# One pass over all tokens in eight time phases, with the depthwise conv on full 128x128 matmuls through DRAM

## The reference, cut to what matters

```python
u = rmsnorm(h, g_mix)                       # 2176 tokens x 1024 per core
proj = einsum('ntd,de->nte', u, w_in)       # 1024 -> 9216, nine parts of 1024
s  = a_c * a_h                              # branch A, conv over 3 tokens
ya = (a_b * dwconv3(s) * silu(a_z)) @ w_out_a
v  = b_v * sigmoid(b_g)                     # branch B, conv over 31 tokens
c  = dwconv31(v) + b_conv_b
yb = (silu(layernorm(c)) * silu(b_z)) @ w_out_b
m  = sigmoid(gate_a) * ya + sigmoid(gate_b) * yb
h  = h + m @ w_o
h  = h + sigmoid(rmsnorm(h, g_ple) @ w_pg) * (p @ w_pe)
y  = rmsnorm(h, g_final)
```

## Time and profile before

| | us |
|---|---|
| median of the runs (1200.08 to 1239.26) | 1201.93 |
| the profiled execution, its own time | 1197.04 |
| its span on the slowest core, first to last instruction | 1195.5 |
| spans of the eight cores | 1174.0 to 1195.5 |

### The profile page before, as it was taken

The page is one execution under the profiler, slowest core; times in us unless marked ns, Lnnn a source line. Parts: engine busy times, 40 slices in busy tenths (PEclk is TensorE's granted clock), DMA queues, the critical chain, the costliest instruction groups (busy, mean ns, idle before and its releaser), DMA issues.

```text
span 1195.5 us, 20798 instructions; the slowest of 8 cores (1174.0 to 1195.5 us)
## 1 busy us (share of the span) xinstructions
PE 1022.0 (85%) x6774; PEld 571.8 (48%) x6774; DVE 560.9 (47%) x927; ACT 356.6 (30%) x661; POOL 230.1 (19%) x512
## 2 busy tenths in 40 slices
PE   1599979989899876999988989988689978789984
PEld 1355555545466333555654546633355544445542
DVE  1334325666333454443665633345646466642354
ACT  3122231332211454223223221135422322331243
POOL 3111011212122122111221212112222222222010
PEclk9788878989999996999999989998799999989998
DMA  8675465536466342545554545543356455477221
GB/s 202 103 139 95 83 151 124 88 55 103 78 103 97 88 120 79 97 87 127 89 87 73 93 75 97 97 109 99 92 114 129 90 102 90 77 151 127 49 87 62
DMA packets 65307, 119.74 MB, mean 100 GB/s; under 512 B 8657, under 2 KB 23377, under 8 KB 64657
## 3 DMA queue, kind: packets, MB, share of 16 engines
q0 software_dynamic: 41184, 75.06, 39.3%
q1 hardware_dynamic: 24017, 43.36, 11.7%
HBM read 172.23 MB, written 11.14 MB: 153 GB/s over the span
## 4 chain that ended last, share of the span: by engine, by line
PE 66%; DVE 11%; issue 8%; ACT 7%; DMA 6%; SPq 0%; DVEq 0%; POOL 0%; ACTq 0%; POOLq 0%
PE ps L687 13%; PE ps L571 11%; PE ps L790 10%; PE ps L508 9%; PE ps L891 6%; PE ps L779 5%; PE ps L784 5%; PE ps L643 3%; DMA t_R<-t_vext 3%; PE ps L844 3%; DMA t_xs<-x 2%; ACT t_tmp L661 2%; DVE t_cbuf L663 2%; DVE t_tmp L653 2%; DVE t_tmp L721 1%
## 5 line engine op out<-in xcount | busy, mean ns | idle before, releaser
L687 PE MATMUL ps<-t_uT,t_ring 128*128 128x512 bf16 (+2 forms) x1536 | 259.3, 332 | 40.4 <-ACT t_tmp L661 23.2
L687 PEld LDWEIGHTS ps<-t_uT,t_ring 128*128 128x128 bf16 x1536 | 145.2, 102 | 152.9 <-issue 66.0
L288 POOL DMA_DIRECT2D t_ring<-w_in x216 | 115.7, 536 | 500.0 <-PE ps L508 228.5
L571 PE MATMUL ps<-t_R,t_Wp 128*64 128x512 bf16 (+2 forms) x1536 | 141.9, 341 | 15.8 <-DMA t_R<-t_vext 15.7
L508 PE MATMUL ps<-t_uT,t_ring 128*128 128x512 bf16 (+2 forms) x768 | 136.5, 336 | 0.3 <-DVE t_uT L426 0.3
L790 PE MATMUL ps<-t_uT,t_ring 128*128 128x512 bf16 (+2 forms) x768 | 129.5, 322 | 0.0
L571 PEld LDWEIGHTS ps<-t_R,t_Wp 128*64 128x64 bf16 x1536 | 84.2, 116 | 71.3 <-issue 34.1
L891 PE MATMUL ps<-t_wpg_t,t_u2T 128*128 128x512 bf16 x272 | 74.0, 434 | 31.5 <-DVE t_u2T L867 22.5
L508 PEld LDWEIGHTS ps<-t_uT,t_ring 128*128 128x128 bf16 x768 | 70.2, 102 | 63.2 <-issue 32.0
L790 PEld LDWEIGHTS ps<-t_uT,t_ring 128*128 128x128 bf16 x768 | 71.1, 99 | 51.0 <-issue 5.4
L801 DVE TENSOR_TENSOR t_tmp<-ps,t_tmp 128x512 f32<-128x512 f32 (+2 forms) x48 | 25.6, 534 | 123.9 <-ACT t_tmp L797 123.9
(11 more groups left out here) (119 smaller groups left out, 1125.3 us busy)
## 6 DMA issues: line engine op xcount, KB each, us to landing
t_ring<-w_in POOLq DMA_DIRECT2D x216, 256.0 KB, 5.2
t_xs<-x SPq DMA_DIRECT2D x34, 512.0 KB, 4.5
y<-t_yt SPq DMA_DIRECT2D x17, 512.0 KB, 2.7
t_R<-t_vext SPq DMA_DIRECT2D x96, 67.8 KB, 2.0
t_ring<-w_oa POOLq DMA_DIRECT2D x24, 256.0 KB, 4.0
t_ring<-w_ob POOLq DMA_DIRECT2D x24, 256.0 KB, 4.7
t_R<-t_vexts SPq DMA_DIRECT2D x32, 76.0 KB, 4.1
t_R<-t_vext SPq DMA_DIRECT2D x64, 35.8 KB, 3.8
```

The costliest lines, as they stand in the source:

```text
L288: S.add("pool", lambda e, k=k, src=src: e.dma_start(out=ring[k].rearrange("p k m -> p (k m)"), in_=src), writes=[f"ring{k}", swq()], dma=f ...
L571: S.add("pe", lambda e, bc=bc, ds=ds, i=i, g=g, rhs=rhs, n=n: e.matmul(ps[64 * g:64 * g + 64, bc, 0:n], lhsT=Wp[ds][:, 16 * g + i, :], rhs ...
L687: S.add("pe", lambda e, b=b, kw=kw, k=k, off=off, n=n: e.matmul(ps[:, b, 0:n], lhsT=ring[kw][:, k, :], rhs=uT[:, k, off:off + n], start=(k ...
```

## The change

All 2176 tokens go through each stage together, in five chunks (`CHUNKS`), so each weight tile is loaded once. The host lays the 2048 prompt tokens out in eight phases: token 8m + a stands at column 256a + m. A shift by eight tokens is then a shift by one column within a phase.

The long conv works on `v8`, whose 128 partitions are 16 channels x 8 phases. For 16 channels, one 128 x 128 matrix per lag (five lags) maps the eight phases of the input to the eight of the output; 64 such groups of channels times five lags make 320 matmuls of 336 columns (256 of the prompt, 80 of the short sequences with their histories). VectorE builds the matrices from a table `tw` and a block mask, four groups at a time (`w_build`). v is written to DRAM with channels as rows (`vd`, `vsd`), read back as 16 channels x 8 phases (`conv_load`), and the result makes the same way back (`cd`, `csd`, `conv_back`). The sums for the LayerNorm are then made from the result (`acc`), and the conv bias is added where it is used.

The tile of short sequences comes first. The first four channel groups are projected chunk by chunk while token tiles arrive; the other four alternate with halves of the conv. Branch A's short conv takes its earlier tokens from the phase before, so chunk 3 comes first in each j. b_z chunks stand behind j = 2 to 7. The last stage runs over 17 token tiles with more buffers, u2T of the next tile ahead of the products of this one. Each accumulation now waits for its own bank. p, and the histories, come transposed from the host; kept rows go out untransposed. The float32 identity, the halos and their copies are gone. SBUF is laid out by hand, with tiles of late stages over those of early ones (`alias` carries the waits).

The diff at its core:

```diff
+NPH = 8
+NBL = 256
+NQ = 8
+NLAG = 5
+NWIN = 336
+CHUNKS = [(0, 512), (512, 512), (1024, 512), (1536, 512), (2048, 128)]
...
+            add_group([wcol(5, j), wcol(4, j)])
...
+        TILES = [16] + list(range(16))
+        def s1_load(i):
+            t = TILES[i]
+            sdma(xs1[i % NXS][:], x_d[128 * t:128 * t + 128, :], [], [f"x1{i % NXS}"], f"x1{i % NXS}")
+        s1_load(0)
+        sdma(vecs[:], vecs_d, [], ["vecs"], "vecs")
+        for i in range(1, NXS):
+            s1_load(i)
+        pdma(idb[:], ident_d, [], ["idb"], "idb")
+        pump(2)
+        S.add("pool", lambda e: e.memset(mhalf[:], -0.5), writes=["mhalf"])
+        pump(6)
+        pdma(tw.rearrange("p a b -> p (a b)"), tw_d, [], ["tw"], "tw")
+        pdma(mask[:], mask_d, [], ["mask"], "mask")
+        S.add("pool", lambda e: e.memset(epsc[:], LN_EPS), writes=["epsc"])
...
+        def s2_proj(j, si):
+            off, n = CHUNKS[si]
+            if j not in s2w:
+                s2w[j] = wgroup()
+            g, (kg, kv) = s2w[j]
+            bg, bv = balloc(), balloc()
+            proj(bg, kg, si)
+            proj(bv, kv, si)
+            tg = talloc()
+            S.add("act", lambda e: e.activation(out=tmp[tg][:, 0:n], in_=ps[:, bg, 0:n], func=AF.Sigmoid),
+                  reads=[f"ps{bg}"], writes=[f"tmp{tg}"])
+            if si < 4:
+                q = vst_ctr[0] % NVST
+                vst_ctr[0] += 1
+                S.add("dve", lambda e: e.tensor_tensor(out=vst[q][:], in0=ps[:, bv, :], in1=tmp[tg][:], op=ALU.mult),
+                      reads=[f"ps{bv}", f"tmp{tg}"], writes=[f"vst{q}"])
...
+                sdma(vd[j][:, off:off + n], vst[q][:], [f"vst{q}"], [f"vd{j}_{si}"], f"vst{q}")
+            else:
+                S.add("dve", lambda e: e.tensor_tensor(out=vkeep_s[:, j, :], in0=ps[:, bv, 0:n], in1=tmp[tg][:, 0:n],
+                                                       op=ALU.mult),
+                      reads=[f"ps{bv}", f"tmp{tg}"], writes=[f"vkeep_s{j}"])
+                pdma(vsd[j], vkeep_s[:, j, :], [f"vkeep_s{j}"], [f"vsd{j}"], f"vsd{j % 4}")
+            bfree(bg, bv)
+        def conv_load(j):
+            s = j % 2
+            pdma(v8[s][:, :, 260:340], h8_d[j], [], [f"v8{s}h"], f"v8{s}h")
+            sdma(v8[s][:, :, 4:260], vd[j].rearrange("c (a m) -> (c a) m", m=NBL).rearrange("(q r) m -> r q m", r=128),
+                 [f"vd{j}_{si}" for si in range(4)], [f"v8{s}p"], f"v8{s}p")
+            sdma(vs8[s][:], vsd[j].rearrange("c (a m) -> (c a) m", m=16).rearrange("(q r) m -> r q m", r=128),
+                 [f"vsd{j}"], [f"vs8{s}"], f"vs8{s}")
+            S.add("pool", lambda e: e.tensor_copy(out=v8[s][:, :, 264:340:5], in_=vs8[s][:]),
+                  reads=[f"vs8{s}"], writes=[f"v8{s}h"])
+        def w_build(j, hh):
+            w = (2 * j + hh) % NWP
+            c0 = (j * NQ + 4 * hh) * NLAG
+            S.add("dve", lambda e: e.tensor_tensor(
+                out=Wp[w].rearrange("p a (c b) -> p a c b", b=NPH),
+                in0=mask.rearrange("p (c b) -> p c b", b=NPH).unsqueeze(1).to_broadcast([128, 4 * NLAG, 16, NPH]),
+                in1=tw[:, c0:c0 + 4 * NLAG, :].unsqueeze(2).to_broadcast([128, 4 * NLAG, 16, NPH]), op=ALU.mult),
+                reads=["tw", "mask"], writes=[f"Wp{w}"])
...
+        def conv_half(j, hh):
+            s, w = j % 2, (2 * j + hh) % NWP
+            for pr in range(2):
+                b0, b1 = balloc2()
+                for u, b in enumerate((b0, b1)):
+                    qq = 2 * pr + u
+                    q = 4 * hh + qq
+                    for d in range(NLAG):
+                        S.add("pe", lambda e, b=b, qq=qq, q=q, d=d: e.matmul(
+                            ps[:, b, 0:NWIN], lhsT=Wp[w][:, qq * NLAG + d, :], rhs=v8[s][:, q, 4 - d:4 - d + NWIN],
+                            start=(d == 0), stop=(d == NLAG - 1)),
+                            reads=[f"Wp{w}", f"v8{s}z", f"v8{s}p", f"v8{s}h"], writes=[f"ps{b}"])
+                x = c8_ctr[0] % NC8
+                c8_ctr[0] += 1
+                q0 = 4 * hh + 2 * pr
+                S.add("act", lambda e, b0=b0, b1=b1, x=x: e.activation(out=c8[x][:], in_=two(b0, b1, 0, NBL),
+                                                                       func=AF.Copy),
+                      reads=[f"ps{b0}", f"ps{b1}"], writes=[f"c8{x}"])
+                S.add("act", lambda e, b0=b0, b1=b1, q0=q0: e.activation(out=c8s[s][:, q0:q0 + 2, :],
+                                                                         in_=two(b0, b1, 260, NWIN, 5), func=AF.Copy),
+                      reads=[f"ps{b0}", f"ps{b1}"], writes=[f"c8s{s}"])
+                bfree(b0, b1)
+                rows = cd[j].rearrange("c (b m) -> (c b) m", m=NBL).rearrange("(q r) m -> r q m", r=128)
+                sdma(rows[:, q0:q0 + 2, :], c8[x][:], [f"c8{x}"], [f"cd{j}_{q0}"], f"c8{x}")
+            if hh == 1:
+                sdma(csd[j].rearrange("c (b m) -> (c b) m", m=16).rearrange("(q r) m -> r q m", r=128), c8s[s][:],
+                     [f"c8s{s}"], [f"csd{j}"], f"c8s{s}")
+            k = 2 * j + hh + NWP
+            if k < 2 * NCH:
+                w_build(k // 2, k % 2)
+        def conv_back(j):
+            if j == 4:
+                S.alias([f"c{q}_{si}" for q in range(4, 8) for si in range(5)], X1_RES)
+            sdma(cb[:, j, 0:2048], cd[j], [f"cd{j}_{q}" for q in (0, 2, 4, 6)], [f"c{j}_{si}" for si in range(4)],
+                 f"cb{j % 2}")
+            sdma(cb[:, j, 2048:NTOK], csd[j], [f"csd{j}"], [f"c{j}_4"], f"cbs{j % 2}")
...
+        def s6_Cpe(t):
+            x = t % 2
+            g0, g1 = balloc2()
+            e0, e1 = balloc2()
...
+            rs_ap, rs_res = s6[t]
+            S.add("act", lambda e: e.activation(out=B[x].rearrange("p (h d) -> p h d", h=2), in_=two(g0, g1, 0, 512),
+                                                func=AF.Sigmoid, scale=rs_ap),
+                  reads=[f"ps{g0}", f"ps{g1}", rs_res], writes=[f"B{x}"])
+            bfree(g0, g1)
+            return e0, e1
+        def s6_Cend(t, eb):
+            e0, e1 = eb
+            x, q = t % 2, t % 3
+            bv = B[x].rearrange("p (h d) -> p h d", h=2)
+            S.add("dve", lambda e: e.tensor_tensor(out=bv, in0=two(e0, e1, 0, 512), in1=bv, op=ALU.mult),
+                  reads=[f"ps{e0}", f"ps{e1}", f"B{x}"], writes=[f"B{x}"])
+            bfree(e0, e1)
+            S.add("dve", lambda e: e.tensor_tensor(out=B[x][:], in0=B[x][:], in1=A[q][:], op=ALU.add),
+                  reads=[f"B{x}", f"A{q}"], writes=[f"B{x}"])
...
+        s1_stats(0)
+        s1_stats(1)
+        s1_rest(0)
+        w_build(0, 0)
+        nxt = [1]
+        def s1_next():
+            i = nxt[0]
+            if i >= len(TILES):
+                return
+            nxt[0] += 1
+            if i + 1 < len(TILES):
+                s1_stats(i + 1)
+            s1_rest(i)
+        for j in range(4):
+            s2_proj(j, 4)
+            s1_next()
+        for si in range(4):
+            for j in range(4):
+                s2_proj(j, si)
+                if si == 3:
+                    wdone(s2w[j][0])
+                s1_next()
+                if si == 0 and j < NWP - 1:
+                    w_build((j + 1) // 2, (j + 1) % 2)
+                if si == 3 and 1 <= j < 3:
+                    conv_load(j - 1)
+        jobs = [(j, si) for j in range(4, 8) for si in range(5)]
+        halves = [(j, h) for j in range(NCH) for h in range(2)]
+        hk = [0]
+        accd = [0]
+        def half():
+            j, h = halves[hk[0]]
+            hk[0] += 1
+            conv_half(j, h)
+            if h == 0 and j >= 1:
+                conv_back(j - 1)
+            if h == 1:
+                if j + 2 < NCH:
+                    pend.append(j + 2)
+                if j >= 2:
+                    acc(j - 2)
+        pend = []
+        for i, (j, si) in enumerate(jobs):
+            s2_proj(j, si)
+            if si == 4:
+                wdone(s2w[j][0])
+            while pend and (pend[0] < 4 or pend[0] < j or (pend[0] == j and si == 4)):
+                conv_load(pend.pop(0))
+            while hk[0] < 14 and 1.25 * hk[0] + 1 <= i:
+                half()
+        while hk[0] < 14:
+            half()
+        while pend:
+            conv_load(pend.pop(0))
...
+        NT = NTOK // 128
+        for t in range(NT):
+            eb = s6_Cpe(t)
+            if t + 2 < NT:
+                s6_p(t + 2)
+            if t + 1 < NT:
+                s6_B(t + 1)
+            s6_Cend(t, eb)
+            if t + 2 < NT:
+                s6_A(t + 2)
+            if t + 3 < NT:
+                s6_x(t + 3)
+            s6_out(t)
```

1234 lines of the change are left out of this document (517 added, 717 removed).

## The result

The changed kernel takes 1025.26 us (median of four runs: 1016.22, which is the profiled one, 1018.01, 1032.51 and 1038.43). Without the executions that a low clock on part of the cores made longer, the ratio to the kernel before is 0.8537, with a 95% interval of 0.8267 to 0.8807. The interval is wide because the kernel before ran only four times beside it, with 1182.69 as the lowest; beside the later experiments it took 1183.06 to 1188.58 us in 21 of 22 runs, so the change is worth about 168 us. The direction was right and the time lies in the range, which is 170 us wide, but 972 was too low: the profiled span is 1014.7 us where the sum said 968.

A forecast was written before the change was run, and what follows sets the result against it. TensorE, busy 85% of the span, was taken as the bound. Work 855 + start 42 + conv path 16 + statistics 5 + z chain 10 + last stage and tail 15 + clock 25 = 968 us span, forecast 972, range 905 to 1075.

The forecast's parts named there:

- the sum of columns: TensorE work of the whole kernel, added up from matmul rates: 855 us in the new kernel, 949 in the old.
- The build's price: One Wp build of 2560 elements on VectorE: 2.9 us, or 1.5 if 16-bit inputs double the rate.
- the entry: Entry into the last stage: a loss of 5 us, beside 10 for the tail.
- the start: Before dense projections: VectorE's first build waits for the table, first 512-column projection at about 47 us, loss 42.
- 35 against 37 for j 2 to 5, hidden: Gated conv with one z tile per j: 35 us of VectorE against 37 of matmul, so no loss.
- what eight banks absorb: Gated conv with z: eight PSUM banks reduce the loss of 14 us, from j 6 and 7, to 10.
- the conv stage: Projections of j 4 to 7 beside conv halves: 14.1 us per j, plus a loss of 16, from 0 to 84.
- The price per group: DMA time of the conv's path through DRAM: 16 to 26 us per j, against 14.1 of matmul.
- this path sets its stage: Rival: the conv's DRAM path takes 26 us per j, seven j cost 83, total about 1040; chance 0.19.
- the clock: Whole run: 25 us kept for a low granted clock on the slowest core.
- the second rival: Low clock of 0.81 for most of the run: 1144 throughout, about 1070 for half the run; chance 0.14.
- Weights once: Weights loaded once instead of three times, 88 DMAs for 264: worth nothing alone, as the load already hides.

The follow-up runs named there:

- w_late: Changed kernel with the first conv weight build emitted after the first 512-column projection instead of before the short sequences' projections: 1012.81 us (one run).
- start_both: As w_late, and POOL issues six weight tiles, the table and the mask after the statistics of the first two token tiles: 1082.56 and 1002.67 us.
- z_piped: Changed kernel with each b_z chunk's last product emitted behind VectorE's first two operations of the next chunk: 994.14 us (median of three runs).
- pace: Changed kernel with ScalarE, in the first stage, scaling tile i before it squares tile i+1: 1014.57 us (one run).
- all_in: Changed kernel with the edits of z_piped, pace and start_both, and histories loaded as contiguous rows: 947.68 us (median of four runs).
- before_z: Kernel before the change, with each b_z chunk's last product behind the next chunk's first two VectorE operations: 1142.47 us profiled, 1238.81 in a second run.

## Why the prediction was right or wrong, step by step

**Right: the sum of columns.** The old kernel's 247 us beside its 949 of matmul became 160 beside 855. So of 181 us of span 94 are columns, as forecast, and 87 are waits and slow matmuls, where the forecast had 134. The build's price, left open between 1.5 and 2.9 us, is decided: 1.489 us for 2560 elements, 16 times, the lower bound. The last stage ran at 8.2 us a tile (two L762 at 871.24 and 879.46 us), the entry cost 5, as said.

**Wrong by 5: the start.** The chain was named in full (POOL's issues, the table, the build on VectorE, `vkeep_s`, the statistics), but the tiles that should "follow each other at about 2.5 us" came 4.45 us apart: transposes at 40.34, 44.79 and 49.24. The build was shorter than its 2 to 3 us, so the two partly cancel, by luck. w_late gave back 5 us at that point, start_both 13.

**Wrong by 20: a step that was not there.** The sum gave the first projections of j 0 to 3 only their columns and transposes. I never laid a token tile's ScalarE work (0.60, 1.24, 1.14 us) beside one job. The new order puts a tile into each of twelve jobs of 3.56 us, and from the start of the sigmoid to the end of the scaled copy ScalarE needs 2.7 us (60.65 to 63.32), which begin 2 us into the job. ScalarE's share is 31%, and it was still what TensorE waited for. The reordering gave back 15 of the 20; the last tile of a chunk costs about the rest (L391 on uT, 6.0 us of the list's 7.5 in this stage).

**Wrong by 26: "35 against 37 for j 2 to 5, hidden".** The chain is where the sum failed most. The 3.64 us of chain were right. But TensorE waited 3.1 to 3.6 us on each b_z tile of j 2 to 5, where the step says nothing; behind j 2 it was:

```profile
390.65 1.89 PE L391 MATMUL ps<-t_uT,t_ring 128*128 128x512 bf16 x8 [1.16 <-ACT t_tmp L708]
394.29 1.89 PE L391 MATMUL ps<-t_uT,t_ring 128*128 128x512 bf16 x8 [1.76 <-ACT t_tmp L708]
396.50 33.47 PE L391 MATMUL ps<-t_uT,t_ring 128*128 128x512 bf16 x184 [0.32 <-ACT t_tmp L708]
```

TensorE makes a b_z tile in 7.4 us, the chain empties it in 16.4, and eight banks do not hold the difference; what VectorE has free in the next 29 us cannot give it back. In the sum the term was 10, all for j 6 and 7; it measured 35.9, 13.1 for j 2 to 5 and 22.8 for j 6 and 7 with two tiles each. Half of the miss is thus the step called hidden, and half the "what eight banks absorb". An average over a j is the wrong test for a burst. The old kernel's wait in the earlier trace rows was the very same thing, and removing it gave 44 us in one kernel and 45 in the other: this cost was never part of the change. The prediction booked some 80 of the old 247 us to this stage, with the LayerNorm among them, and kept 10 of it for the chain.

**Wrong by 11: the conv stage, 16 for 27.** The loss is 20.0 us of waiting and 6 of matmuls at the 1.2 GHz level behind them (5.40, 5.45 and 4.56 us for 20, against 3.02), and 7.2 more at the seam, which the table has a row lower. The step "v8 is loaded two halves and two or three jobs ahead (some 10 us), and is hidden unless that traffic queues" held its own condition: it queued. The price per group was well bounded: 0.84 of 140 us is 118 us of DMA, 17 for each of seven groups, in the forecast's 16 to 26, and groups came every 18.4 us. The rival, that this path sets its stage, so happened in kind, at 18 of its 68 us more, seam included. Its cause, small packets, is not borne out for the histories' rows: a quarter fewer software packets gave 2 us, and the same packets earlier gave 16 us. For the other small packets it stays open. The Trainium skill (DMA: Bandwidth & Descriptors, Why small descriptors are slow) puts a cost on small descriptors with HBM. No run here contradicts that cost, but for these 160 B rows it is no more than the 0.6 us between median landings of 8.0 and 7.4.

**Wrong by 25: the clock.** The term was taken from one core of one run, and this low clock did not come back in the profiled execution: 0.967 on the slowest core. That the term compensated a third of the missing waits is luck. Another cost of the clock was there and was not in the sum, the 21 us at the 1.2 GHz level behind waits; it stands in the stages' excess above.

The low clock of the second rival is real, but did not come in this execution. In z_piped cores 2 and 3, in pace cores 0 and 1 had 0.72 to 0.79 from 180 to 300 us, and core 3 of z_piped had 0.81 without a single wait from 290 to 330. It also takes a whole die for a whole span: in one execution of all_in the four cores of die 0 had 0.825 to 0.832 and 1093.86 us, 147 us more than its three others at the median, and die 0 of a start_both (1082.56 us) had 0.862 to 0.880, die 1 of a before_z (1238.81 us) 0.850 to 0.853. The Trainium skill (TensorE: Matmul & The Clock Gate, Part 1) has the whole die at 13/16 once three of its cores run dense matmuls. The value agrees with the 0.81; the condition does not decide it here, since from 300 to 340 us of the changed kernel all eight cores ran matmuls for 39.8 of 40 us or more at a clock of 1.00. What picks no core, two cores or a whole die stays open.

**Weights once: nothing,** as said. The output stage, where a weight is used for 2176 columns and DMA is at 0.31 of its time against 0.58, runs at the old rate. I did not test it alone, nor the new conv without the one pass, so the shares of the two in the 171 us rest on the rates.

**Slips in the working.** The low clock for half the run is 1043 us by the prediction's own terms (half of 855 at 0.81, plus 88); its 1070, near the upper end of the range, also holds the 25 of the sum. 969.5 times 1.004 is 973, not 972. Of the packets of the earlier trace rows only the hardware queue's were between two tiles on the chip; the 1436 of the software queue were weights. And the old shifted copies did not land quite unhindered after the start: TensorE waited for them three more times, 6.3 us together on core 3 after 60 us.

## What to carry to other kernels

Test a burst against the buffers that must hold it, not an average: where the bound engine outruns a chain for one tile, its wait is lost even if the other engines have time later. When a change reorders stages, list what every engine does for one job of each new pairing, also an engine that is busy 31% of the time. And issue a load that depends on nothing ahead of whatever its queue waits for; the size of its rows mattered less here than its place.
